# A two-block network on one core: rotation table, S5 fetches, norm sums and tile order moved

## The reference

```python
# NSA: compressed, selected and sliding-window attention, 16 heads of 64
o = gate0 * softmax(q kc^T - slope*d) vc + gate1 * softmax(q ks^T - slope*d) vs + gate2 * softmax(q kw^T - slope*d) vw
x = x + (o * silu(z)) @ w_out
# S5: per group a complex diagonal recurrence over the sequence, 16 channels, 64 states
u, z = split(rmsnorm(x) @ w_in);  s_t = a * s_{t-1} + B u_t;  y = gelu(Re(C s_t) + d_skip * u)
x = x + (ga(y) * sigmoid(gb(y)) * silu(z)) @ w_out
# second block: retention, gated linear attention (GLA), sliding-window attention (SWA)
m = sum over n of sigmoid(h @ w_bgate[n]) * (branch_n(h) @ w_branch[n])
x = x + rmsnorm(m @ w_o) * g
x = x + rmsnorm((silu(rmsnorm(x) @ w_fg) * (rmsnorm(x) @ w_fu)) @ w_fd) * g     # 2816 wide
```

## Time and profile before

| | |
|---|---|
| median of 3 runs | 1976.67 us (1976.65 to 1977.06) |
| profiled execution, its own time | 1976.76 us |
| span of its instructions | 1974.9 us |
| TensorE busy | 1830.2 us, 93% |
| VectorE busy | 968.0 us, 49% |
| ScalarE busy | 853.2 us, 43% |
| GpSimd busy | 194.4 us, 10% |

### The profile page before, as it was taken

The page is one execution under the profiler, slowest core; times in us unless marked ns, Lnnn a source line. Parts: engine busy times, 40 slices in busy tenths (PEclk is TensorE's granted clock), DMA queues, the critical chain, the costliest instruction groups (busy, mean ns, idle before and its releaser), DMA issues.

```text
span 1974.9 us, 24065 instructions
## 1 busy us (share of the span) xinstructions
PE 1830.2 (93%) x9758; PEld 1464.3 (74%) x9758; DVE 968.0 (49%) x1622; ACT 853.2 (43%) x1437; POOL 194.4 (10%) x318
## 2 busy tenths in 40 slices
PE   6899999699889999997999999999899789999996
PEld 4677777479878877875687777877787568888884
DVE  7878456454754354244345445345544454344223
ACT  6445666445354234234345553355623443222222
POOL 2000226710000000000000000022200021111000
PEclk9999999899999999999999999999999879999998
DMA  4554331035142323311232222211132112232331
GB/s 134 171 185 132 100 107 44 1 102 202 65 155 85 101 82 116 96 44 43 84 93 70 84 70 91 89 64 64 54 100 86 61 64 97 95 103 87 99 93 57
DMA packets 60319, 181.29 MB, mean 92 GB/s; under 512 B 7008, under 2 KB 18080, under 8 KB 57776
## 3 DMA queue, kind: packets, MB, share of 16 engines
q1 hardware_dynamic: 60208, 179.75, 28.0%
HBM read 165.57 MB, written 16.25 MB: 92 GB/s over the span
## 4 chain that ended last, share of the span: by engine, by line
PE 73%; DVE 11%; ACT 7%; POOL 4%; issue 2%; DMA 1%; SPq 0%; DVEq 0%; ACTq 0%; POOLq 0%
PE bank L886 18%; PE bank L887 17%; PE bank L888 17%; PE bank L925 2%; PE bank L927 2%; PE bank L926 2%; DVE wlo L1906 2%; PE bank L1067 1%; POOL Ps L2661 1%; ACT Ps L1804 1%; PE bank L1088 1%; ACT whi L1357 1%; ACT L1362 1%; PE bank L906 1%; PE bank L908 1%
## 5 line engine op out<-in xcount | busy, mean ns | idle before, releaser
L1906 DVE TENSOR_TENSOR wlo<-wraw,whi 128x1024 fp32r<-128x1024 f32 (+1 forms) x262 | 316.7, 1211 | 332.2 <-ACT whi L1357 330.9
L886 PE MATMUL bank<-Hh,whi 128*128 128x512 f32 (+2 forms) x1104 | 446.3, 404 | 16.4 <-DVE wlo L1906 16.3
L887 PE MATMUL bank<-Hl,whi 128*128 128x512 f32 (+2 forms) x1104 | 435.0, 394 | 0.0
L888 PE MATMUL bank<-Hh,wlo 128*128 128x512 f32 (+2 forms) x1104 | 434.8, 394 | 0.0
L1357 ACT ACTIVATE whi<-wraw 128x1024 fp32r<-128x1024 f32 (+1 forms) x262 | 271.5, 1040 | 313.1 <-PE bank L888 239.7
L886 PEld LDWEIGHTS bank<-Hh,whi 128*128 128x128 f32 (+2 forms) x1104 | 208.6, 189 | 75.0 <-DVE wlo L1906 14.1
L888 PEld LDWEIGHTS bank<-Hh,wlo 128*128 128x128 f32 (+2 forms) x1104 | 208.5, 189 | 46.8 <-issue 0.6
L887 PEld LDWEIGHTS bank<-Hl,whi 128*128 128x128 f32 (+2 forms) x1104 | 208.6, 189 | 45.4 <-issue 2.2
L1362 ACT ACT_TABLE_LOAD x97 | 124.5, 1283 | 2.8 <-DVE epst L1921 1.1
L886 PE MATMUL bank<-Bh,whi 128*128 128x512 f32 x256 | 103.5, 404 | 2.2 <-DVE Bl L2435 2.2
L887 PE MATMUL bank<-Bl,whi 128*128 128x512 f32 x256 | 102.6, 401 | 0.0
(11 more groups left out here) (360 smaller groups left out, 3064.2 us busy)
## 6 DMA issues: line engine op xcount, KB each, us to landing
wraw<-in_w_o SPq DMA_DIRECT2D x24, 512.0 KB, 3.4
wraw<-in_w_bgate SPq DMA_DIRECT2D x24, 512.0 KB, 3.4
wraw<-in_w_branch SPq DMA_DIRECT2D x24, 512.0 KB, 3.4
wraw<-in_w_fg SPq DMA_DIRECT2D x22, 512.0 KB, 3.4
wraw<-in_w_fu SPq DMA_DIRECT2D x22, 512.0 KB, 3.5
wraw<-in_w_glu SPq DMA_DIRECT2D x16, 512.0 KB, 3.5
wraw<-in_w_fd SPq DMA_DIRECT2D x16, 512.0 KB, 3.5
scratch_CA<-CA SPq DMA_DIRECT2D x4, 1152.0 KB, 6.2
```

The costliest lines, as they stand in the source:

```text
L886: pe.matmul(o, wh[:, cols], hi(k), start=k == 0, stop=False)
L887: pe.matmul(o, wh[:, cols], lo(k), start=False, stop=False)
L888: m = pe.matmul(o, wl[:, cols], hi(k), start=False, stop=k == K - 1)
L1906: dve.tensor_tensor(c.wlo[q][:, 0:n], c.raw[i % RR][:, 0:n], c.whi[q][:, 0:n].bitcast(F32), S_).then_inc(*up(DID, ("wlo", i)))
```

## The change

Five pieces:

- **A.** In the attention GpSimd makes parts 0 to 3 of the rotation table, in passes 28, 30, 32 and 34 (before: 34, 38, 42 and 46). Parts 4 and 5, 18 instructions of 128x512, are VectorE's, one in each pass from 38 to 55 (before: GpSimd's, in passes 50 and 54).
- **B.** The bank `kk` is given back after `store_k` and no longer right after `prep_k`. For 14 later steps another bank results.
- **C.** In S5 the fetches of `mW` 2, `mW` 3, `mCA`/`mT` 2 and 3 stand earlier.
- **D.** At the feed-forward's start `post` of block k+1 stands between `resid` and `split_h3` of block k; the squares go to `sqb` and TensorE sums them with one matmul of ones per block (`sum_h3`), in place of seven additions on GpSimd and one sum; and the products of the first two tiles stand block by block in the same loop (`lead`).
- **E.** At the retention's end the products `w_ga`, `w_g` 0 and `w_g` 4 stand between the last product, the means, the sum of squares and the fence; their evictions follow the fence.

```diff
@@ Plan.attention
-            if i >= AWAY + 6 and (i - AWAY) % 4 == 2 and (i - AWAY - 6) // 4 < 6:
-                self.step("prep_r", (i - AWAY - 6) // 4)
+            if i in range(AWAY, AWAY + 8, 2):
+                self.step("prep_r", (i - AWAY) // 2)
+            if i in range(AWAY + 10, AWAY + 28):
+                self.step("prep_r_wide", *divmod(i - AWAY - 10, 6))
@@ Plan.prep
             self.step("prep_k", b)
-            self.bank.give(("kk", b))
             for n in range(3):
                 self.step("prep_w", b, 1, n)
                 if n == 2:
                     self.step("store_k", b)
+                    self.bank.give(("kk", b))
@@ Plan.s5
-        order = ("a0 b0 m1 a1 e0 b1 r0 a2 s0 b2 r1 a3 s1 r2 b3 w2 o0 s2 z0 r3 t0 o1 w3 m2 z1 s3 y0 t1 z2 o2 m3 y1 z3 t2 "
+        order = ("a0 b0 m1 a1 e0 b1 r0 a2 s0 w2 b2 r1 a3 s1 w3 r2 b3 o0 m2 s2 z0 r3 t0 o1 m3 z1 s3 y0 t1 z2 o2 y1 z3 t2 "
                  "o3 y2 z4 t3 y3 z5 z6 z7")
@@ Plan.second
-        for k in range(KT + 1):
-            if k < KT:
-                self.step("post", "o2", k)
-            if k:
-                self.step("resid", "o2", k - 1)
-                self.step("split_h3", k - 1)
-                self.square("h3", k - 1, 0, k == 1, by="pool")
+        keys, at = self.leading([("w_fg", 0), ("w_fu", 0)], "h3")
+        self.bank.take(("total", "h3"))
+        self.step("post", "o2", 0)
+        for k in range(KT):
+            self.step("resid", "o2", k)
+            if k < KT - 1:
+                self.step("post", "o2", k + 1)
+            self.step("split_h3", k)
+            self.sqb.take(("sq", "h3", k))
+            self.step("square_h3", k)
+            self.sqb.give(("sq", "h3", k))
+            self.step("lead", keys, at, k)
+            self.step("sum_h3", k)
@@ Plan.retention
-        self.tick()
+        self.drain()
+        self.gemm("w_ga", 0, "h2", M=16)
         next(post)
-        self.tick()
+        self.gemm("w_g", 0, "h2")
         next(post, None)
-        self.drain()
+        self.gemm("w_g", 4, "h2")
         self.step("fence", 3)
@@ Plan.gla
-        self.gemm("w_ga", 0, "h2", M=16)
-        self.evict(("w_ga", 0))
+        for key in (("w_ga", 0), ("w_g", 0), ("w_g", 4)):
+            self.evict(key)
 ...
-        heads(0)
         self.step("gla_in")
@@ Plan.ffn
-        self.pair([("w_fg", 0), ("w_fu", 0)], "h3")
-        self.inv("h3", 0, 7, 0, 1.0 / D, "rs")
+        self.step("inv", "h3", 0, 1.0 / D, "rs")
+        self.bank.give(("total", "h3"))
@@ tensor
+    def sum_h3(k):
+        key = ("sq", "h3", k)
+        if k == 0:
+            on.wait_ge(*before(plan.bank, ("total", "h3")))
+        on.wait_ge(*at(*key))
+        pe.matmul(bank(("total", "h3")), c.ones[:, :], c.sqb[plan.sqb.of[key]], start=k == 0, stop=k == KT - 1).then_inc(
+            *up(PE, ("freed", key), *([("total", "h3")] if k == KT - 1 else [])))
@@ scalar
+    def square_h3(k):
+        key = ("sq", "h3", k)
+        on.wait_ge(*at("x3", k))
+        on.wait_ge(*before(plan.sqb, key))
+        act.activation(c.sqb[plan.sqb.of[key]], c.X[:, k, :], ACT.Square).then_inc(*up(DID, key))
@@ vector
+    def prep_r_wide(part, n):
+        w, b0, b1 = [(16, 0, 4), (32, 0, 2), (32, 2, 4)][part]
+        R = lambda i, n0, n1: c.Rh[:, b0:b1, i, :, n0:n1]
+        last = lambda i: c.Rh[:, b0:b1, i, :, w - 1:w].broadcast_to([128, b1 - b0, 8, w])
+        t1, t2 = [x[:, :].rearrange("p (b q n) -> p b q n", q=8, n=w) for x in c.tR]
+        on.wait_ge(*at("Rs"))
+        if n in (0, 3):
+            tt(t1, R(0, 0, w), last(n // 3), M)
+        elif n in (1, 4):
+            tt(t2, R(1, 0, w), last(1 - n // 4), M)
+        else:
+            tt(R(n // 5, w, 2 * w), t1, t2, A_ if n == 5 else S_, *([("Rh",)] if (part, n) == (2, 5) else []))
```

More of the change, by code:

```diff
@@ L163, in pair, with leading @@
         self.step("pair", keys, at)
+    def leading(self, keys, src):
+        for key in keys:
+            self.tiles[key] = (src, KT, 128)
+            self.bank.take(key)
+        return keys, [self.piece(w, (col,), 0, 1024) for w, col in keys]
     def tok(self, w, m, n, kper, src, between=iter(())):
@@ L191, in square @@
             self.sqb.take(key)
-        self.step("square", gen, k, acc, first, by)
+        self.step("square", gen, k, acc, first)
         if not first:
@@ L910, in pair, with lead @@
                     m.then_inc(*up(PE, ("used", i), ("tile", key)))
+    def lead(keys, pieces, k):
+        hi, lo = c.moving[plan.tiles[keys[0]][0]]
+        cols = slice(k * 128, k * 128 + 128)
+        on.wait_ge(*at("lo", plan.tiles[keys[0]][0], k))
+        for key, i in zip(keys, pieces):
+            o = bank(key)
+            wh, wl = c.whi[plan.ring[i]], c.wlo[plan.ring[i]]
+            if k == 0:
+                on.wait_ge(*before(plan.bank, key))
+                on.wait_ge(*at("wlo", i))
+            pe.matmul(o, wh[:, cols], hi(k), start=k == 0, stop=False)
+            pe.matmul(o, wh[:, cols], lo(k), start=False, stop=False)
+            m = pe.matmul(o, wl[:, cols], hi(k), start=False, stop=k == KT - 1)
+            if k == KT - 1:
+                m.then_inc(*up(PE, ("used", i), ("tile", key)))
+    def sum_h3(k):
+        key = ("sq", "h3", k)
+        if k == 0:
+            on.wait_ge(*before(plan.bank, ("total", "h3")))
+        on.wait_ge(*at(*key))
+        pe.matmul(bank(("total", "h3")), c.ones[:, :], c.sqb[plan.sqb.of[key]], start=k == 0, stop=k == KT - 1).then_inc(
+            *up(PE, ("freed", key), *([("total", "h3")] if k == KT - 1 else [])))
     def tok(keys, i, j, n, kper, src):
@@ L1330, in wd @@
         x.then_inc(*up(PE, ("wd", u), ("wd", u + 1)))
-    walk(plan, dict(mm=mm, pair=pair, tok=tok, tok_twin=tok_twin, rsS=rsS, rows=rows, total=total, hold=hold, fence=fence, cmp_end=cmp_end,
+    walk(plan, dict(mm=mm, pair=pair, lead=lead, sum_h3=sum_h3, tok=tok, tok_twin=tok_twin, rsS=rsS, rows=rows, total=total, hold=hold, fence=fence, cmp_end=cmp_end,
                     vecs=vecs, gate_t=gate_t, cmp_w1=cmp_w1, cmp_out=cmp_out,
@@ L1907, in split_lo, with square @@
             *up(DID, ("wlo", i)))
-    def square(gen, k, acc, first, by):
-        if first or by != "dve":
+    def square(gen, k, acc, first):
+        if first:
             return
@@ L2662, in wb @@
         x.then_inc(*up(DID, ("wn", u)))
-    def square(gen, k, acc, first, by):
-        if first or by != "pool":
-            return
-        key = ("sq", gen, k)
-        on.wait_ge(*at(*key))
-        on.wait_ge(*at("acc", gen, k - 1))
-        gp.tensor_tensor(c.nacc[acc][:, :], c.nacc[acc][:, :], c.sqb[plan.sqb.of[key]], ALU.add).then_inc(
-            *up(DID, ("acc", gen, k), ("freed", key)))
     def ffn(k):
```

31 lines of the change are left out of this document (15 added, 16 removed).

## The result

The changed kernel takes 1921.86 us (median of four runs, 1921.54 to 1924.01), the kernel before 1976.66 beside it. The ratio is 0.9728 with an interval of 0.9711 to 0.9744. The profiled execution took 1921.54 us, with a span of 1919.7. Over all nine runs the median is 1923.6, which I use as the reference for the experiments.

What follows compares the result with a forecast made beforehand. TensorE, at work nearly everywhere in fixed order, bounds the kernel, so time comes only from its stalls. Gains of 14 + 5.9 + 15.5 + 8 + 12 = 55.4 us take 1976.7 to 1921.3, rounded 1921; range 1911 to 1936.

Steps and rivals of the forecast that it cites:

- upper bounds of A and D: Largest gains allowed: 20 us for the attention's rotation table, 9 us for the feed-forward's start.
- One sign that I had named for being wrong: Attention: eight-unit cycles exceeding 23 us would above all show the forecast wrong.
- the first and the last term: Attention: the first of four eight-unit cycles was forecast at about 22.2 us, the last at 17.6.
- the second too large: Attention: the second eight-unit cycle, with eight rotations on VectorE, was forecast at about 20.3 us.
- over 95% busy: Attention: VectorE, setting the pace, would be over 95% busy in the second and third cycles.
- Rival 1: Attention: VectorE's rotations wait for GpSimd's instructions; the rotation table gains only 5 us, total 1930; chance 0.17.
- rival 3: S5 and retention's end: waits pass to the states' chain and `ro` copies; gains 11 and 9, total 1929; chance 0.12.
- The term that was mis-sized: Retention's end: the means would run at full clock, 1.9 us and not 3.78.
- Rival 2: Feed-forward's start: TensorE stays at half clock, blocks 4.3 us, −6 instead of +8, total 1935; chance 0.08.

Runs made afterwards that it cites:

- undo_a: Changed kernel with GpSimd making all six parts of the rotation table again, in passes 34 to 54; 1934.52 us.
- one_input: Changed kernel with ten of VectorE's eighteen wide products replaced by row sums reading one operand (table wrong); 1925.46 us.
- d_pool: Changed kernel keeping the feed-forward's new `post` order and block-by-block products, but squares added by GpSimd as before; 1929.08 us.
- undo_b: Changed kernel with the bank `kk` given back right after its product again; 1933.60 us.
- undo_c: Changed kernel with the four S5 fetches back at their old places in the order string; 1937.89 us.
- undo_e: Changed kernel with `w_ga`, `w_g` 0 and `w_g` 4 behind the fence again at the retention's end; 1935.04 us.
- e2: Changed kernel with `w_g` 0 moved in front of the means and `w_g` 4 in front of the sum of squares; 1921.26 us.
- undo_d: Changed kernel with the feed-forward's start as before: old `post` order, GpSimd adding the squares, no block-by-block products; 1931.79 us.

## Why the prediction was right

Forecast 1921, measured 1921.9 and, over nine runs, 1923.6; the range of 1911 to 1936 held. All five mechanisms came as told, each shown by its own undoing, but the closeness of the first set's total is partly luck: A and E brought 1.6 and 1.2 us less than forecast, B, C and D together 1.1 more, and some 1.5 us of the lead lie between the pieces. The working of the range has a slip: the upper bounds of A and D and half of the other three's come to 1913; 1911 takes all five in full. Point by point:

- **A, 14 forecast, 12.4 in the lining up, 11 to 13 by `undo_a`.** The mechanism was right: GpSimd's parts go, VectorE becomes the pace. One sign that I had named for being wrong did appear: a stretch of over 23 us. The first took 23.7 us and not 22.2, because parts 1 to 3, pushed together, left waits of 1.1, 1.5, 0.7 and 0.5 us behind them and one short stretch at the lower clock (0.93); the last took 19.4 and not 17.6. The second took 18.4 and not 20.3. So the first and the last term were too small by 1.5 and 1.8 us and the second too large by 1.9. The eighteen products lie 7, 8 and 3 in the three stretches, where I had counted 8, 8 and 2. VectorE is not over 95% busy as I said, but 83 and 88%: it is late at single places, not throughout. Rival 1 (rotations that wait for GpSimd) is out: 0.70 us at the median, 0.94 at most, and with one operand (`one_input`) the stretches are as long. The rule of the Trainium skill that I weighed there (SBUF — State Buffer, Who interferes with whom) agrees with the trace where the two start together, as the 1.77 us of `d_pool` show; in the attention most of the delay is GpSimd's, some 2 us per stretch, and costs 1.1 us at most in the three.
- **B, 5.9 forecast, 6.2 in the lining up and by `undo_b` at the place.** Right there, both the wait and the slow matmuls behind it, which cost 1.8 and not 1.5. That its undoing cost 10 us in the whole wasn't foreseen, and the 3.8 us beyond the place are open.
- **C, 15.5 forecast, 15.8 in the lining up, 14.3 by `undo_c`.** The terms came: two waits and the slow stages, of which the third (4.87 against 3.71) didn't return in `undo_c`. Behind them TensorE waits only twice, 0.9 us together, for `Yo`, so rival 3 doesn't hold for C.
- **E, 12 forecast, 10.8 in the lining up, 11.4 by `undo_e`.** The term that was mis-sized is the clock after the wait for `ro`: behind 2.42 us of waiting the means took 2.76 us and not 1.9, and the first product behind them 1.42. That is the half of rival 3 that holds. I had taken both at the upper clock. `e2` takes the wait away and gets them.
- **D, 8 forecast, 8.5 in the lining up, 8.2 by `undo_d`.** VectorE's 2.14 and TensorE's 2.24 us per block came as worked out, the first block's start at the lower clock too. Rival 2 (lower clock throughout) is out: the blocks after the first two run at 2.24.
- **The sum.** 55.4 forecast; 54.8 with the first set, 53 with all nine runs. What I hadn't priced is that the same program scatters over 5 us, more than any of my errors by piece.

## What to carry to other kernels

When one engine is at work over 90% of the time, list its stalls with what ended each, and price each edit as the stall plus the work behind it that ran at the lower clock. A stall of 4.4 us was worth 6.2, and stalls of 11.4 us in S5 were worth 15.8. After an engine's long block is broken up, look at what stands in front of the next one in the same queue: small parts packed together made the stretch 23.7 us long, spreading them made it 18.8, and 3 us of that were left in the whole attention.

An addition that GpSimd does "for free" beside VectorE's two-operand instructions isn't free: one of 1.32 us cost VectorE 1.1 us here. TensorE with a matrix of ones did it for 0.86 us, in a place where it would mostly have waited.

A version should be judged at the edited place first, by lining up the traces, and by the total only if the effect is above the program's own scatter.
